# The stores of 24 partial results per layer are begun by GpSimd instead of the sync engine

## What is computed

```python
for l in range(2):
    h = rms_norm(x, ln_g[l])
    qa, ka, va, ga, qb, kb, vb, gb, qc, kc, vc, gc = split(h @ w_in[l])
    ya = window_sink_attention(...)          # mixer A, +-128 tokens
    yb = global_axial_attention(...)         # mixer B, dense
    yc = dilated_mixture_attention(...)      # mixer C, three dilations
    x = x + concat(ya*silu(ga), yb*silu(gb), yc*silu(gc)) @ w_out[l]
# in mixer C, for the groups g = 0, 1, 2 (dilations 1, 4, 16):
#   outs[g] = softmax_g @ v_g ; lses[g] = logsumexp of the scores
#   y = sum_g softmax(lses)[g] * outs[g]
```

## Time and profile before

| | |
|---|---|
| median of the three runs | 2781.38 us |
| lowest and highest | 2779.66 and 2786.03 us |
| the profiled execution | 2778.55 us |
| its span in the trace | 2776.3 us |
| PE busy | 2745.0 us, 99% of the span |
| POOL busy | 940.0 us, 34% |
| stores `part_rows<-part_out` | 48, 132 KB each, from 660.0 to 2099.6 us |

### The profile page before, as it was taken

How to read it: one execution, slowest core, us unless ns; L and a number is a source line. 1 busy time by engine, 2 the same in 40 slices (tenths; PEclk the granted TensorE clock), 3 DMA queues, 4 the chain that set the end, 5 groups by cost and what they waited for, 6 DMA issues and landing times. The chain is left out here.

```text
span 2776.3 us, 44022 instructions
## 1 busy us (share of the span) xinstructions
PE 2745.0 (99%) x14817; PEld 2465.0 (89%) x14817; DVE 1616.3 (58%) x3973; ACT 1218.3 (44%) x3017; POOL 940.0 (34%) x860
## 2 busy tenths in 40 slices
PE   8999999999999999999999999999999999999999
PEld 7888899989999999988888888999899999998887
DVE  3345644434676777677743465444256767776776
ACT  4322222225665566544542222222266655665443
POOL 0333433320465377500003334333105743774000
PEclk9999999999999999999999999999999999999999
DMA  5366656569554442464524565656694455325535
GB/s 176 107 185 196 185 180 192 175 178 240 144 136 123 127 113 82 156 234 129 198 90 134 180 191 176 194 174 187 177 254 131 115 129 144 96 69 213 195 122 182
DMA packets 422202, 444.65 MB, mean 160 GB/s; under 512 B 64119, under 2 KB 316183, under 8 KB 421980
## 3 DMA queue, kind: packets, MB, share of 16 engines
q1 hardware_dynamic: 421980, 441.84, 53.5%
HBM read 315.93 MB, written 125.80 MB: 159 GB/s over the span
## 5 line engine op out<-in xcount | busy, mean ns | idle before, releaser
L1706 ACT CAST w_hi<-w_raw 128x512 fp32r<-128x512 f32 x640 | 396.7, 622 | 699.5 <-PE bank L1489 428.7
L1973 DVE TENSOR_TENSOR w_lo<-w_raw,w_hi 128x512 fp32r<-128x512 f32 x640 | 457.0, 715 | 398.8 <-ACT w_hi L1706 394.8
L1487 PE MATMUL bank<-w_hi,act_hi 128*128 128x512 f32 x1728 | 688.9, 399 | 0.0
L1489 PE MATMUL bank<-w_hi,act_lo 128*128 128x512 f32 x1728 | 679.0, 393 | 0.0
L1488 PE MATMUL bank<-w_lo,act_hi 128*128 128x512 f32 x1728 | 677.6, 392 | 0.0
L2388 POOL TENSOR_SCALAR prob<-prob,denom 128x256 f32<-128x256 f32 (+2 forms) x288 | 348.3, 1214 | 246.4 <-DVE denom L2104 243.1
L1489 PEld LDWEIGHTS bank<-w_hi,act_lo 128*128 128x128 f32 x1728 | 372.5, 216 | 54.1
L1487 PEld LDWEIGHTS bank<-w_hi,act_hi 128*128 128x128 f32 x1728 | 373.3, 216 | 50.2
L1488 PEld LDWEIGHTS bank<-w_lo,act_hi 128*128 128x128 f32 x1728 | 373.1, 216 | 48.6
L1543 PE MATMUL bank<-act_hi,w_hi 128*128 128x384 f32 x1024 | 346.7, 339 | 0.0
L1545 PE MATMUL bank<-act_hi,w_lo 128*128 128x384 f32 x1024 | 344.6, 337 | 0.0
(11 more groups left out here) (123 smaller groups left out, 4617.8 us busy)
## 6 DMA issues: line engine op xcount, KB each, us to landing
w_raw<-w_in SPq DMA_DIRECT2D x144, 512.0 KB, 4.6
w_sums<-sum_out SPq DMA_DIRECT2D x32, 1280.0 KB, 6.7
w_raw<-w_sums SPq DMA_DIRECT2D x80, 512.0 KB, 4.1
sum_in<-w_out SPq DMA_DIRECT2D x64, 512.0 KB, 5.7
heads_t<-turned SPq DMA_DIRECT2D x240, 128.0 KB, 2.4
q_t<-heads_t SPq DMA_DIRECT2D x192, 128.0 KB, 2.1
k_t<-keys_t SPq DMA_DIRECT2D x48, 384.0 KB, 5.6
w_raw<-w_out SPq DMA_DIRECT2D x32, 512.0 KB, 3.9
```

The source lines that it names most:

```text
L1487: pe.matmul(acc[t][:], hi, w_hi[:, W_AT[n]:W_AT[n] + SLAB], start=(k == 0), stop=False)
L1489: last = pe.matmul(acc[t][:], lo, w_hi[:, W_AT[n]:W_AT[n] + SLAB], start=False, stop=(k == KC - 1))
L1706: nc.scalar.copy(w_hi[:, W_AT[n]:W_AT[n] + SLAB], w_raw[:, load % W_RAW, j, :]).then_inc(w_hi_done, 1)
L1973: nc.vector.tensor_tensor(w_lo[:, W_AT[n]:W_AT[n] + SLAB], w_raw[:, load % W_RAW, j, :], w_hi[:, W_AT[n]:W_AT[n] + SLAB].bitcast(F32), ALU ...
```

## The change

GpSimd begins the 48 stores. The table that placed them in SP's list is gone. In GpSimd's list the store of quad `q` stands in turn `q + 5`, the turn in which DVE copies that part, behind the scaling of that turn and ahead of the merges and gates. The wait for `part_taken`, the data, the addresses and the semaphores of the slots are as before.

```diff
-PARTS_AT = at_items((i, x["step"] + MIX_LAG) for i, x in enumerate(ITEMS) if x["kind"] == "Q")
...
                     if it < N_ITEMS:
                         load_item(l, it)
-                    for i in PARTS_AT.get(it, ()):
-                        store_part(l, i)
                     for u in KEYS_AT.get(it, ()):
...
+            def store_part(l, it):
...
+                q = l * N_QUADS + item["quad_no"]
+                pool.wait_ge(part_taken, q + 1)
...
+                pool.dma_start(dst, part_out[:, q % PART_SLOTS, :, :].rearrange("p h n -> p (h n)"))\
+                    .then_inc(part_stored[q % PART_SLOTS], 16)
...
                     if 0 <= i - NORM_LAG < N_STEPS and features_first(STEPS[i - NORM_LAG]):
                         normalise(l, i - NORM_LAG)
+                    if ends_quad(i - MIX_LAG):
+                        store_part(l, STEPS[i - MIX_LAG]["item"])
                     for mc, stage in merge_turns(i, PARTS_TURN, 2):
```

More of the change, by code:

```diff
@@ L1265, in store_sums @@
                 sp.dma_start(w_sums[:, j, :, h * SLAB:(h + 1) * SLAB].rearrange("i p c -> p i c"), sum_out[:]).then_inc(sums_stored, 16)
[L1267 to L1278, removed]
             def load_x(l, s):
@@ L2409, in gate_product @@
                 nc.gpsimd.tensor_tensor(v, v, gate_t[:, at % GATE_SLOTS, tokens], ALU.mult).then_inc(gated, 1)
+            def store_part(l, it):
+                item = ITEMS[it]
+                unit = item["unit"]
+                q = l * N_QUADS + item["quad_no"]
+                pool.wait_ge(part_taken, q + 1)
+                first, step = token_order(item["t"], True)
+                row = 2 * KV_C * 2 * PART
+                dst = bass.AP(part_rows.tensor, first * row + ((unit["g"] - 1) * KV_C + unit["j"]) * 2 * PART,
+                              [[step * row, P], [1, 2 * PART]])
+                pool.dma_start(dst, part_out[:, q % PART_SLOTS, :, :].rearrange("p h n -> p (h n)"))\
+                    .then_inc(part_stored[q % PART_SLOTS], 16)
             def merge_back(l, mc, stage):
```

## The result

The change made the kernel slower by a third of a per cent: 2791.82 us in the median of 12 runs (2786.34 to 2797.29), against 2780.64 us (2779.38 to 2786.03, 12 runs) of the kernel before. The ratio is 1.0034, with an interval from 1.0027 to 1.0042. The forecast was 2780.4 us with 2777.5 to 2787.0.

The account below looks back on a forecast made before the run. PE was taken as the bound, busy 2745.0 of 2776.3 us. The profiled 2778.55 - 0.96, other terms 0, gave 2777.6 us; as that execution lies 2.83 us under the median, the forecast was 2780.4 us, range 2777.5 to 2787.

Parts of the forecast that it names:

- What the change removes: SP's queue behind a change of keys and biases: item 17's load issued 0.48 us earlier per layer, -0.96 us in all.
- Rival 2: Quad turns: stores served earlier delay each load behind a change of keys and biases 0.53 us; +3.2 us, 2784.6 us, chance 0.12.
- The price on POOL: POOL's time to begin one store, c, taken as 1.0 us and hidden in a turn of 2.62 us.
- Rival 1: POOL's own time for a store, deciding from c = 2.55 us; at 3.0 us, 2798 us; chance 0.06.
- The Trainium skill's rule on GpSimd's descriptors: GpSimd can't write descriptors while DVE runs a copy using both its ports; by this c would be 3.5 us.
- The last four stores: Stores between POOL's scalings, behind each of which a scaling waits that PE transposes; hidden at 1.0 us, cost 0.
- The last landing: Last store before DVE's first addition into `mixed_t` at 727.45: lands 1.3 us early, at worst 0.3 us late; cost 0.
- DVE's waits: DVE's 12.5 us of waits for stores in the quad turns should nearly go, and be worth 0 to PE.
- the marks of 2 and 5 us: DVE's wait for `part_rows`: under 2 us, stores land in time; 5 or more, DMA engines set the landing.
- The sign that was named: PE busy in the two 52 us windows: 51.4 or more, as forecast; below 50.5, rival 2.

Follow-up runs that it names:

- the later one: The changed kernel measured again beside the kernel before, on another chip: 2786.44 us against 2781.38 us, ratio 1.0011.
- three stores ahead on SyncE: The kernel before, with the stores of quads 2, 8 and 14 begun by SyncE ahead of the item's load: ratio 1.0008, then 1.0009 (2783.76 us).
- the first ScalarE run: The kernel before, with the stores of quads 2, 8 and 14 begun by ScalarE at the end of its turn: 2793.01 us, ratio 1.0030.

## Why the prediction was wrong

**What the change removes** is the step that failed. It took the load of item 17 to be issued 0.48 us earlier and to land 0.48 us earlier, -0.96 us in all. In layer 0 it was issued 0.06 us earlier: the keys began 0.26 us earlier (678.73 for 678.99), and the biases took 2.32 us in the queue for 2.12. PE's wait for it stayed at 0.80 us. In layer 1 that wait grew from 0.59 to 2.50 us, and the load of item 11, for which PE had not waited, cost 0.79 and 0.88 us. The term measured about +2.4 to +3.6 us of waits of PE (3.8 and 5.0 us in the two profiles, for 1.4), the wrong sign.

**Rival 2, the loads lose to the stores,** is what happened. One reason against it was misread. "The stores of before lay ahead of the same loads" is true of quad 7's but not of quad 8's, which stood behind the load of item 17, at 683.15 for 682.29. The change moved one store of each burst, those of quads 2, 8 and 14, from behind the load to beside the burst, and these six carry the loss. Its price was 0.53 us for each of six loads, +3.2 us. For the waits alone the sum was near: the span without half clock is 2.8 us longer. That is in part luck, since three loads became later for PE, by 0.79, 0.88 and 1.91 us, and not six by 0.53. What the rival lacked is the second step, the granted clock that falls behind a wait. No term of the sum had it, and I had put the rival within 0.2% by itself, with a chance of 0.12. The half clock adds 5.1 us in the profiled run, and at the median run's 0.996, where the profiled one had 0.998, about as much again (an estimate from the listed clocks). That carried the time out of the range in one measurement; in the later one, at 1.0011, it is inside.

**Whether PE's queries are late by the second queue as such** the runs answer as likely in part: landings of up to 9.1 to 9.8 us with six stores in GpSimd's or ScalarE's queue, and up to 8.0 to 8.1 with the same six in SyncE's. But PE waits 4.2 to 4.5 us in all with those too, so their place near the burst makes most of the waits, and the second queue the longest ones. The Trainium skill (DMA: Bandwidth & Descriptors, Issuing engines are not separate DMA queues) says that DMAs of all the issuing engines run on the same 16 engines and interleave there. The landings agree that a second queue is no lane of its own; what it costs the loads of the first, one to two microseconds for 132 KB, no run here takes apart.

**The price on POOL**, c = 1.0 us, was 0.54 us in the quad turns, and 0.60 between the scalings. Rival 1 (from 2.55 us on) is out. The Trainium skill's rule on GpSimd's descriptors (SBUF — State Buffer, SBUF: two separate sides), by which an estimate had been 3.5 us, shows no sign here: no POOL store took over 0.772 us. **The last four stores** cost nothing: PE is busy for 27.00 of 27 us behind the quad turns, as before. **The last landing**: the first addition into `mixed_t` begins at 727.69 without a wait for a store, 0.24 us behind its time of before. **DVE's waits** fell from 12.5 to 3.7 us, and to 5.8 in the later profile, between and above the marks of 2 and 5 us that were named: the stores come sooner, yet the DMA engines hold them up in part. That these waits were hidden was right: PE's waits for DVE are 0.3 us in each layer, before and after.

**The sign that was named** read true: it was a PE busy below 50.5, rival 2, and the busy time is 50.12 and 48.34 us.

Open stay three things: what makes the loads behind a burst land later when a second queue is in use; why three stores ahead on SyncE are no gain where all ahead are (1.0009 and 0.9984); and at which of several small waits the clock falls.

A version beats both kernels by a little: all stores on SyncE ahead of their loads, 0.9987 and 0.9984 on two chips. The change with its bias tiles one item later reached 0.9981 on a third.

## What to carry to other kernels

Ask of each DMA that moves to another queue which load with no slack it now travels beside, not how long its bytes take; here it was the loads behind a burst, and six stores of 48 decided. A change that lengthens waits of a TensorE that is 99% busy is priced twice, once for the wait and once for the half clock behind it, which was larger here (5.1 us for 2.7) and comes in some executions only. Where the clock column varies from run to run, compare on one chip, count the executions with a lower clock, and look at a profile with and one without the stretch. And a control that moves one thing is worth more than a fitting number: three stores ahead on SyncE showed that most of the waits need no second queue.

## What the runs showed of the hardware

- A PE that had been idle for 2.50 us, and in another kernel for 0.78 us of 4 in two pieces, was granted 0.50 of its clock for about 10 us behind it. In other executions waits of 1.5 us, and one of 2.4 us in layer 0 of the first ScalarE run, left it at 1.00. So the length of a single wait doesn't tell it. The same kernel had such a stretch in some executions only: on one chip 18 of 33 of the kernel before list a mean clock under 1.000.
- Six writes of 128 single floats cost the kernel 34 to 42 us, from GpSimd or from SyncE.
- A DMA of 132 KB begun by GpSimd held POOL for 0.54 us, and by ScalarE its sequencer for 0.33 to 0.35 us. GpSimd's 48 stores went in 2304 packets, 48 for each, where SyncE's had been 144 each:

```profile
q0 software_dynamic: 2304, 6.49, 0.6%
```
